# Layer norm of a one-core decoder layer: the mean and reciprocal deviation applied on GpSimd instead of ScalarE and VectorE

## What is computed

```python
def layer_norm(t, gain, bias):
    tf = t.astype(jnp.float32)
    mu = jnp.mean(tf, axis=-1, keepdims=True)
    var = jnp.mean(jnp.square(tf - mu), axis=-1, keepdims=True)
    return (tf - mu) * lax.rsqrt(var + LN_EPS) * gain.astype(jnp.float32) + bias.astype(jnp.float32)

y = jnp.concatenate([rms_normalize(oa), rms_normalize(ob), rms_normalize(oc)], axis=-1)
y = y * g_branch * jax.nn.silu(z)
y = jnp.einsum('bse,ed->bsd', y, w_out)
x = layer_norm(DEEPNORM_ALPHA * x + y, ln_gain, ln_bias)
```

## Time and profile before

| | us |
|---|---|
| median of 3 runs | 500.43 (500.07 to 501.27) |
| profiled execution, whole | 500.67 |
| its span, first to last instruction | 498.5 |
| outside the span | 2.17 |
| PE busy | 488.8 (98%) |
| DVE busy | 311.0 (62%) |
| ACT busy | 226.6 (45%) |
| POOL busy | 70.8 (14%) |

### The profile page before, as it was taken

One profiled execution on the slowest core, in us unless ns is written; L12 is line 12 of the kernel. 1 busy time (PEld: TensorE's weight loads), 2 busy tenths in 40 slices (PEclk: granted clock), 3 DMA queues, 4 the chain that ended last, 5 costly groups with the idle time before them and its releaser, 6 DMA issues.

```text
span 498.5 us, 9771 instructions
## 1 busy us (share of the span) xinstructions
PE 488.8 (98%) x3526; PEld 448.3 (90%) x3526; DVE 311.0 (62%) x893; ACT 226.6 (45%) x511; POOL 70.8 (14%) x52
## 2 busy tenths in 40 slices
PE   8999999999999999999999999999999999999994
PEld 7999999999999988888888888899888898888883
DVE  4878644557565853434534468876767868877734
ACT  5632222112211134564545659947374656454540
POOL 0000000000000000111101100023232323231414
PEclk9999999999999999999999999999999999999998
DMA  7984453547632344532331258723333424232022
GB/s 283 376 255 127 159 180 104 193 134 248 212 126 87 105 125 131 158 99 75 95 97 50 98 164 266 233 58 104 114 101 106 135 68 151 67 116 83 1 85 84
DMA packets 51838, 67.97 MB, mean 136 GB/s; under 512 B 9552, under 2 KB 41296, under 8 KB 51792
## 3 DMA queue, kind: packets, MB, share of 16 engines
q1 hardware_dynamic: 51216, 66.31, 41.6%
q10 hardware_dynamic: 576, 1.05, 0.6%
HBM read 51.31 MB, written 16.02 MB: 135 GB/s over the span
## 4 chain that ended last, share of the span: by engine, by line
PE 90%; DVE 3%; ACT 3%; DMA 1%; issue 1%; SPq 0%; DVEq 0%; ACTq 0%
PE long_ps L1032 16%; PE o_ps L979 10%; PE wide L846 8%; PE wide L845 8%; PE wide L844 8%; PE narrow L961 5%; PE long_ps L921 5%; PE long_ps L923 5%; PE long_ps L922 5%; PE wide L949 4%; PE wide L950 3%; PE wide L855 2%; PE wide L857 2%; PE wide L856 2%; DMA x_raw<-in_x_t 1%; PE narrow L1008 1%
## 5 line engine op out<-in xcount | busy, mean ns | idle before, releaser
L846 PE MATMUL wide<-x_hi,w_lo 128*128 128x256 f32 x320 | 89.6, 280 | 0.0
L844 PE MATMUL wide<-x_hi,w_hi 128*128 128x256 f32 x320 | 89.3, 279 | 0.0
L845 PE MATMUL wide<-x_lo,w_hi 128*128 128x256 f32 x320 | 89.3, 279 | 0.0
L845 PEld LDWEIGHTS wide<-x_lo,w_hi 128*128 128x128 f32 x320 | 60.2, 188 | 0.0
L846 PEld LDWEIGHTS wide<-x_hi,w_lo 128*128 128x128 f32 x320 | 60.1, 188 | 0.0
L1113 ACT ACTIVATE spill<-turn 128x512 fp32r<-128x512 f32 x21 | 13.3, 632 | 102.7 <-DVE turn L1349 76.6
L844 PEld LDWEIGHTS wide<-x_hi,w_hi 128*128 128x128 f32 x320 | 59.8, 187 | 0.0
L1622 POOL TENSOR_TENSOR g_lo<-g_raw,g_hi 128x1024 fp32r<-128x1024 f32 x6 | 14.3, 2387 | 268.5 <-ACT g_hi L1118 268.5
L1032 PE MATMUL long_ps<-wo_hi,y_hi 128*128 128x512 f32 (+1 forms) x128 | 52.2, 408 | 0.0
L1032 PE MATMUL long_ps<-wo_lo,y_hi 128*128 128x512 f32 (+1 forms) x128 | 51.4, 402 | 0.0
L1032 PE MATMUL long_ps<-wo_hi,y_lo 128*128 128x512 f32 (+1 forms) x128 | 50.8, 397 | 0.0
(11 more groups left out here) (189 smaller groups left out, 1234.4 us busy)
## 6 DMA issues: line engine op xcount, KB each, us to landing
q_spill<-spill SPq DMA_DIRECT2D x32, 256.0 KB, 2.5
q_pair<-q_spill SPq DMA_DIRECT2D x128, 64.0 KB, 2.0
w_raw<-in_w_qkv SPq DMA_DIRECT2D x12, 512.0 KB, 5.0
x_raw<-in_x_t SPq DMA_DIRECT2D x16, 256.0 KB, 8.0
g_raw<-in_w_gate SPq DMA_DIRECT2D x8, 512.0 KB, 4.1
q_pair<-q_spill SPq DMA_DIRECT2D x32, 128.0 KB, 2.8
q_pair<-q_spill SPq DMA_DIRECT2D x128, 32.0 KB, 1.8
wo_raw<-in_w_out SPq DMA_DIRECT2D x8, 512.0 KB, 4.7
```

The source lines that it names most:

```text
L844: pe.matmul(dst, w_hi[s][:, k, f], t_hi[:, k, cols], start=(k == 0), stop=False)
L845: pe.matmul(dst, w_hi[s][:, k, f], t_lo[:, k, cols], start=False, stop=False)
L846: mm = pe.matmul(dst, w_lo[s][:, k, f], t_hi[:, k, cols], start=False, stop=(k == KT - 1))
```

## The change

For blocks 0 to 6, ACT's L1231 and DVE's L1567 go, with the semaphore `ln_shift_ready` and the tile `ln_shift`. POOL gets one operation ahead of its two, a `tensor_scalar` over 128x1024 which subtracts the mean and multiplies with the reciprocal deviation, both read from one column per partition. It waits for `ln_rstd_ready`, which ACT raises in the iteration before. Block 7 is untouched.

```diff
@@ act, iteration NORM_AT[i]
-                    act.wait_ge(ln_shift_ready, i + 1)
-                    act.activation(res[s][:, :], res[s][:, :], ACT.Identity, bias=ln_shift[:, s:s + 1],
-                                   scale=ln_rstd[:, s:s + 1]).then_inc(normed, 1)
@@ dve, iteration NORM_AT[i]
-                    dve.wait_ge(ln_rstd_ready, i + 1)
-                    dve.scalar_tensor_tensor(ln_shift[:, s:s + 1], moments[:, s, 0:1], -1.0, ln_rstd[:, s:s + 1],
-                                             ALU.mult, ALU.mult).then_inc(ln_shift_ready, 1)
@@ pool, iteration NORM_AT[i]
                     if i == 0:
                         pool.wait_ge(ln_in, 32)
+                    pool.wait_ge(ln_rstd_ready, i + 1)
+                    pool.tensor_scalar(res[s][:, :], res[s][:, :], moments[:, s, 0:1], ln_rstd[:, s:s + 1],
+                                       ALU.subtract, ALU.mult).then_inc(normed, 1)
                     pool.wait_ge(normed, i + 1)
                     pool.tensor_tensor(res[s][:, :], res[s][:, :], gain[:, :], ALU.mult).then_inc(gained, 1)
```

More of the change, by code:

```diff
@@ L396, in layer @@
         res_sum, ln_part, ln_stats = sem("res_sum"), sem("ln_part"), sem("ln_stats")
-        ln_logged, ln_rstd_ready, ln_shift_ready = sem("ln_logged"), sem("ln_rstd_ready"), sem("ln_shift_ready")
+        ln_logged, ln_rstd_ready = sem("ln_logged"), sem("ln_rstd_ready")
         normed, gained, finished = sem("normed"), sem("gained"), sem("finished")
@@ L511, in layer @@
         last_stats = small("last_stats", DM // C, 6)
-        ln_log, ln_rstd, ln_shift = small("ln_log", 2), small("ln_rstd", 2), small("ln_shift", 2)
+        ln_log, ln_rstd = small("ln_log", 2), small("ln_rstd", 2)
         assert top <= nc.sbuf_usable_end, top
```

## The result

The changed kernel took 501.88 us (median of 8 runs, 501.48 to 502.40), the kernel before 500.26 (8 runs, 499.88 to 501.27) on the same chip: ratio 1.0031, 95% interval 1.002 to 1.0042. It is slower by 1.6 us, just over the 0.3% that can be told from no change, and above the predicted range. The profiled execution took 502.11 us, its span was 500.0.

A forecast was written before the change was run, and what follows sets the result against it. PE, busy 488.8 of 498.5 us, was taken as the bound. Two waits going, 0.43 + 0.24 = 0.67 us, gave 500.67 - 0.67 = 500.00 for the profiled execution, 499.8 us for the median; range 499.1 to 501.4.

The forecast's parts named there:

- X: Time of each of POOL's seven new 128x1024 operations, which no row showed; estimated at 1.65 us.
- stated bounds of 1.24 and 4.78: Limits in us for POOL's new operation: ACT's time for the same arithmetic, and two POOL two-input operations of 2.39.
- POOL holds DVE off in the tail: Rival: above 1.88 us per POOL operation, DVE's block 7 norm waits; 500.3 us at 2.39; chance 0.20 up to 4.05.
- X - 1.88: Delay of DVE's L1606 in block 7 if POOL's new operation exceeds 1.88 us, going straight to the stores.
- The earlier trace: One overlap near 298 us: POOL, starting during DVE's L1582, lost 0.17 of 0.31 us and DVE none.
- DVE isn't held off at all, SP still is: Tail at 4.78 us per POOL operation: block 6's late store delays block 7's some 0.9 us, 501.3 us.
- gap at 366.03: PE's 0.43 us wait for ACT's probabilities, forecast to close whole; rival that it stays: 500.2 us, chance 0.11.
- wait for `y_lo`: PE's weight-load wait in the tail, forecast to go because `y_hi` starts earlier without L1231; worth 0.24 us.
- Blocks 0 to 5 at price 0: POOL's idle time covers the new operations there; SP's query loads late only beyond 2.36 us per operation.
- limit of 4.2 for `y_lo`: POOL's next `y_lo` behind its norm in blocks 0 to 5 comes no later up to about 4.2 us per new operation.
- gap at 444.21: PE's 0.34 us gap where ACT waited for DVE, counted as 0 gain; rival that more closes: 499.4 us, chance 0.06.

The follow-up runs named there:

- forms: Changed kernel with another form of POOL's first operation in blocks 1 to 5, so their result isn't the layer norm; executed once, for its profile: +1.56 us against before.
- psum_operands: Changed kernel with DVE reading block 7's gain and bias from PSUM, where ACT copies them; 501.94 us (before 500.73), ratio 1.002.
- order_only: Kernel before with only ACT's norm of block 6 put behind the last `y_hi`; 500.69 us (before 500.35), ratio 1.0017.
- kept_in_after: Changed kernel with DVE's small shift operation of block 0 kept, its result unused; 501.47 us (before 500.35), ratio 1.0027.
- half_norm: Changed kernel with POOL norming only columns 0 to 511 of block 6; 500.22 us (before 500.73), ratio 0.999.
- block6_pool: Kernel before with only block 6 normed by POOL's new operation, blocks 0 to 5 as before; 502.31 us, ratio 1.0035.
- longer_norm: Changed kernel with one more POOL operation in block 6, over 512 columns, that changes no value; 504.39 us (before 500.46), ratio 1.0048.
- kept_one: Kernel before with blocks 0 to 5 normed on POOL, block 6 on ACT behind the last `y_hi`, DVE's block 0 shift operation kept unused; 500.70 us (before 500.46), 0.9991.

## Why the prediction was wrong, point by point

- **The cost of X failed.** The step that took a column's cost in proportion to the streams, "If a column's cost goes with the streams (two in place of three), X = ... 1.65 us", had no row behind it. X measured 3.78 us. `forms` shows that fewer inputs don't help (2.77 us for one input and one step, 2.39 for two tensors) and that a second arithmetic step costs 0.9 us more on this tile. 3.78 lay inside the stated bounds of 1.24 and 4.78, and nearer to the upper. That one was put together as two passes of 2.39; measured, one step takes more than such a pass, and the second adds far less.
- **The range was cut inside a rival.** Its upper end, 501.4, holds the case of DVE held by POOL only up to X = 3.3, while that rival itself went to X = 4.05, which by its price is 500.43 + 1.5 = 501.9. No row spoke for 3.3.
- **The rival happened, with the mechanism as put.** "POOL holds DVE off in the tail", which was given 0.20 for X up to 4.05. With X = 3.78 its price is X - 1.88 = 1.90 us, measured 1.68; nearly all of the 0.22 between them is that DVE began 0.20 us before POOL's record ended. With the predicted gains it gives 500.43 - 0.67 + 1.90 = 501.66, against a measured 501.88. That this is so close is partly luck: against the before of the same chip, 500.26, the net is +1.23 by the rival and +1.62 measured. The gains were 0.2 us smaller than predicted, and some 0.3 us came at the very end, which no case had. The earlier trace rows was the right place to look at, but there POOL came second and lost only 0.17 us, so it gave the direction and not the size.
- **Not held, but late stores.** The bound for "DVE isn't held off at all, SP still is" was 0.9 us at X = 4.78. `psum_operands` is this case at X = 3.78. Counted from the last residual addition, block 7's first store is issued 495.47 - 491.95 = 3.52 us later in it and 495.32 - 492.00 = 3.32 before; but the second, which sets the end, comes about 4.0 us later in both (495.9 and 496.0 on their clocks). So waiting for SP costs nothing at this X. What the bound lacked is that the stores land 1.0 us later behind block 6's. That and some 0.3 us at the very end, named below, make up the 1.45 us that the tail is above before. The bound also left out the gap at 366.03, whose 0.43 this case would keep: by the prediction's own terms it is 500.9, not 501.3.
- **The gap at 366.03 closed, as forecast,** and was worth more than its idle time of 0.43: 0.65 us from start to start. For `y_lo` the prediction had counted from start to start, for this gap it had taken the idle time. That is 0.15 us less by the overlap of the records (366.03 - 365.33 = 0.70 in place of 365.80 - 365.68 = 0.12, so 0.58), and 0.07 more was lost at the product behind. The stretch shows 161.33 - 160.58 = 0.75 us for the norms of blocks 0 to 5 without DVE's pause, which is the same within the 0.1 us named above.
- **The wait for `y_lo` went in full and was worth 0.24 us where it stood,** as forecast; in the stretch of `order_only` 0.14 are left of it.
- **A new pause of DVE was in no case of the prediction.** It took back 0.33 us at its place, and 0.42 of the stretch (`kept_in_after` against after).
- **Blocks 0 to 5 at price 0: right, but its limit wasn't tested.** The price was to be "X - 2.36" for SP's query loads beyond X = 2.36. At 3.78 the stores of blocks 2 and 5 were issued 1.3 us late (393.98 against 392.73, 475.27 against 473.95), and PE waited for nothing. But hardly a query load was late: SP had idle time between block 2's store and the next of them (394.44, before 394.55), and behind block 5's store there is none left (the last was at 454.83). The limit of 4.2 for `y_lo` held: POOL still waited 0.41 us for ACT ahead of it.
- **The gap at 444.21 stayed,** as forecast.

The sum, by the places in the trace: -0.65 (gap at 366.03) + 0.33 (DVE's pause) - 0.24 (`y_lo`) = -0.56, against -0.47 in the stretch; the 0.09 between them are the small steps at other products. In the tail +1.68 (DVE held) and some 0.3 at the very end, of 1.97. Together +1.50, and the spans differ by 500.0 - 498.5 = 1.5. The 0.3 is where SP waits for PE's queue (L351), 0.5 us in after and 0.2 before. It is also in `psum_operands`, `half_norm`, `forms` and `kept_in_after`, but not in `block6_pool` or `longer_norm`, and its cause is open.

The best kernel by the traces is `kept_one`: all norms but block 6's on POOL, block 6's on ACT behind the last `y_hi`, 0.95 and 0.93 us below before in its two profiles. Half of that, 0.5 us, is lost outside the span, and in time it can't be told from before (0.9991 and 1.0001).

## What to carry to other kernels

Before work is moved to POOL, find the last operation of that kind before the end of the program and ask which instruction of DVE it would still overlap; an engine with 14% load is free on average, not in the tail. Such a wait appears in no list of waits: compare the duration of each row with its sisters. Count a gap of PE from start to start, not by its idle time. Where an operation's price is unknown, the range has to hold what happens at its upper bound.

## What the runs showed of the hardware

- On POOL a `tensor_scalar` over 128x1024 f32 takes 2.77 us with one step and 3.64 to 3.78 with two, a `tensor_tensor` 2.39, and one with a broadcast second operand 1.89.
- DVE's instruction with two SBUF inputs that became ready while POOL worked waited for the POOL operation in progress, up to some 0.2 us before the end of its record (0.75 us recorded as 2.43 in after); after that they alternated, one instruction each (`longer_norm`). With one of its inputs in PSUM it didn't wait (1.41 us for two, `psum_operands`).
- A store of 256 KB (block 7's halves) landed 2.0 us after its issue with nothing close ahead. Behind one of 512 KB that was issued 0.4 us before it, this was 3.0 us (`psum_operands`), at 1.2 us 2.6 (`longer_norm`), and at 1.9 us (in after) 2.0 again.
- The same instruction of DVE has a pause of 0.28 us ahead of it in eight profiles and none in six, which have one more instruction of 0.15 us earlier in DVE's program, whatever POOL does.
- The time outside the span was near 2.0 to 2.2 us in ten rows of the table and 2.6 to 2.7 in four, in every execution.
- The projections run at two rates at the same granted clock of full speed. Rows of the view by stretch (us, then busy us and count of PE, PEld, DVE, ACT, POOL, granted clock, DMA share, GB/s), of after and then of `kept_in_after`:

```profile
100.00:150.00 50.00, 50.00 (x427) 50.00 (x426) 30.92 (x69) 9.48 (x13) 0.00 (x0) 1.00 0.55 180
```

```profile
100.00:150.00 50.00, 50.00 (x443) 50.00 (x443) 32.44 (x72) 9.49 (x13) 0.00 (x0) 1.00 0.55 180
```

443 matmuls in place of 427 in the same 50 us, 3.7% more. `order_only` has the quick rate too, and executions of before that are 4 us shorter than the rest suggest that it isn't a matter of the change; what sets the rate is open.
